# The pool mixer in plain fp32: averaging and mixer products, token reciprocals on the bands, diagonals on ACT, and the first row broadcast ahead of the second slot

## The reference

```
mods = silu(c) @ ada_w + ada_b ; sh1, sc1, g1, sh2, sc2, g2 = split(mods, 6)     # six rows of 1024
u    = rms_norm(x, mix_pre_g) * (1 + sc1) + sh1
for g, win in enumerate((2, 4, 8, 16)):                                          # 4 groups of 256 channels
    y_g = (centred_window_mean(u_g, win) - u_g) @ pool_w[g]                      # 512x256 @ 256x256
y    = concat(y_g) * pool_scale
x    = x + g1 * rms_norm(y, mix_post_g)
f    = conv_ffn(rms_norm(x, ffn_pre_g) * (1 + sc2) + sh2, ...) ; x = x + g2 * rms_norm(f, ffn_post_g)
```

## Time and profile before

| | us |
|---|---|
| median of 3 runs (1765.6 to 1768.2) | 1767.69 |
| the profiled execution, its own time | 1768.48 |
| its span | 1766.8 |
| PE busy in the span | 1672.8 (95%) |
| DVE busy in the span | 1025.7 (58%) |

### The profile page before, as it was taken

The page is one execution under the profiler, slowest core; times in us unless marked ns, Lnnn a source line. Parts: engine busy times, 40 slices in busy tenths (PEclk is TensorE's granted clock), DMA queues, the critical chain, the costliest instruction groups (busy, mean ns, idle before and its releaser), DMA issues.

```text
span 1766.8 us, 22021 instructions
## 1 busy us (share of the span) xinstructions
PE 1672.8 (95%) x8559; PEld 1402.8 (79%) x8559; DVE 1025.7 (58%) x1649; ACT 643.4 (36%) x1021; POOL 240.8 (14%) x746
## 2 busy tenths in 40 slices
PE   5559999999998999999999999999989999999998
PEld 5448888888877888878888888888878888888886
DVE  6898766676665878857333337666716733333223
ACT  5154433332344766745222222333214522222222
POOL 2001610000017766630000000000010000000000
PEclk7669999999999999999999999999989999999999
DMA  7832222344342222223222234567744232223332
GB/s 289 342 137 96 96 96 95 96 124 145 101 117 81 69 67 69 66 86 111 96 96 96 95 96 132 141 191 228 233 125 132 96 98 101 100 96 96 95 96 72
DMA packets 137783, 211.63 MB, mean 120 GB/s; under 512 B 29920, under 2 KB 104016, under 8 KB 134352
## 3 DMA queue, kind: packets, MB, share of 16 engines
q1 hardware_dynamic: 123024, 203.94, 36.0%
q10 hardware_dynamic: 14656, 6.29, 1.3%
HBM read 192.38 MB, written 17.82 MB: 119 GB/s over the span
## 4 chain that ended last, share of the span: by engine, by line
PE 82%; DVE 9%; DMA 3%; issue 2%; ACT 2%; SPq 1%; POOL 0%; ACTq 0%; DVEq 0%; POOLq 0%
PE bank L1805 26%; PE bank L1806 25%; PE bank L1807 25%; DVE ada L1209 1%; DVE prob L1377 1%; ACT prob L944 1%; DVE w_lo L1113 1%; PE bank L1936 1%; PE bank L1845 1%; PE bank L2226 1%; DVE prob L1392 1%; DMA u_scratch<-us 1%; SPq L676 1%; DMA raw<-in_fox_in 1%; DVE gsig L1363 1%
## 5 line engine op out<-in xcount | busy, mean ns | idle before, releaser
L1805 PE MATMUL bank<-hh,w_hi 128*128 128x512 f32 (+1 forms) x1440 | 553.7, 384 | 6.2 <-DVE w_lo L1113 2.5
L1806 PE MATMUL bank<-hl,w_hi 128*128 128x512 f32 (+1 forms) x1440 | 550.1, 382 | 0.0
L1807 PE MATMUL bank<-hh,w_lo 128*128 128x512 f32 (+1 forms) x1440 | 549.9, 382 | 0.0
L1113 DVE TENSOR_TENSOR w_lo<-raw,w_hi 128x1024 fp32r<-128x1024 f32 x264 | 317.7, 1223 | 190.3 <-ACT w_hi L753 187.9
L753 ACT ACTIVATE w_hi<-raw 128x1024 fp32r<-128x1024 f32 x264 | 277.8, 1056 | 388.5 <-PE bank L1807 127.5
L1805 PEld LDWEIGHTS bank<-hh,w_hi 128*128 128x128 f32 x1440 | 273.2, 190 | 60.9 <-DVE w_lo L1113 4.3
L1807 PEld LDWEIGHTS bank<-hh,w_lo 128*128 128x128 f32 x1440 | 273.0, 190 | 52.3
L1806 PEld LDWEIGHTS bank<-hl,w_hi 128*128 128x128 f32 x1440 | 273.1, 190 | 50.6
L1805 PE MATMUL bank<-w_hi,hid 128*128 128x512 f32 x528 | 206.8, 392 | 0.0
L1807 PE MATMUL bank<-w_hi,hid 128*128 128x512 f32 x528 | 205.6, 389 | 0.0
L1806 PE MATMUL bank<-w_lo,hid 128*128 128x512 f32 x528 | 205.5, 389 | 0.0
(11 more groups left out here) (281 smaller groups left out, 2015.7 us busy)
## 6 DMA issues: line engine op xcount, KB each, us to landing
raw<-in_up SPq DMA_DIRECT2D x132, 512.0 KB, 3.3
raw<-in_dn SPq DMA_DIRECT2D x60, 512.0 KB, 3.9
ada<-in_ada_w SPq DMA_DIRECT2D x24, 1024.0 KB, 6.9
raw<-in_fox_in SPq DMA_DIRECT2D x32, 512.0 KB, 3.4
raw<-in_s_w SPq DMA_DIRECT2D x24, 512.0 KB, 4.2
q_scratch<-q_tab SPq DMA_DIRECT2D x8, 512.0 KB, 4.2
w_scratch<-w_new SPq DMA_DIRECT2D x8, 512.0 KB, 5.1
raw<-in_fox_out SPq DMA_DIRECT2D x8, 512.0 KB, 3.5
```

The source lines that it names most:

```text
L1113: dve.tensor_tensor(w_lo[:, n % RING, :], raw[:, n % RING, :], w_hi[:, n % RING, :].bitcast(F32), ALU.subtract).then_inc(lo_done, 1)
L1805: pe.matmul(dst, w_h, r_h, start=first, stop=False, skip_group_check=True)
L1806: pe.matmul(dst, w_h, r_l, start=False, stop=False, skip_group_check=True)
L1807: return pe.matmul(dst, w_l, r_h, start=False, stop=last, skip_group_check=True)
```

## The change

In the averaging, ACT multiplies the four blocks' bands by the tokens' reciprocals (`band_n`, 128 by 576 each), and PE multiplies `xt` by `band_n` in plain fp32: 32 multiplications. `xr_hi`, `xr_lo`, `band_hi` and `band_lo` are gone. ACT takes the result out as `v` in float32; DVE adds the correction to it. The mixer product multiplies `v` by `raw` in plain fp32, 4 multiplications for each block and slot; the scaled `raw` is used as it is, and the two `hi` and two `lo` of slots 0 and 1 are gone (DVE's scaling now counts up `lo_done`). The two diagonals `diag_gpost1` and `diag_amp2` are made by ACT, in eight instructions each. On PE, `bc(0, ...)` moves from between blocks 1 and 2 of slot 1 to ahead of block 0. On DVE, `early_half(0)` moves behind `modulation(3)` and `scaled(amp2, ...)`.

```diff
                     act.activation(dst[:, HALF * h:HALF * h + HALF], bank[b0 + h][:, :], ACT.Copy).then_inc(bc_done, 1)
+
+            def diagonal(dst, cols):
+                for k in range(KT):
+                    part = act.activation(dst[:, k, :], ident[:, :], ACT.Copy, scale=cols[:, k:k + 1])
+                part.then_inc(diag_done, 1)
 
...
                 prime(ACT.Sqrt)
-                act.wait_ge(band_done, 1)
-                for v in (0, 2):
-                    act.activation(band_hi[:, v, :, :], band_f[:, v, :, :], ACT.Copy).then_inc(bandh_done, 1)
                 for b in range(TB):
...
                 for b in range(TB):
-                    act.activation(xr_hi[:, b, :], xt[:, b, :], ACT.Copy, scale=rn2[:, b:b + 1]).then_inc(xr_done, 1)
-                for n in range(2):
-                    hi(S_POOL + n)
+                    act.activation(band_n[:, b, :, :], band_f[:, BAND_OF[b], :, :], ACT.Copy, scale=rn2[:, b:b + 1])\
+                       .then_inc(bandn_done, 1)
                 act.wait_ge(mod_done, 1)
-                act.wait_ge(bandl_done, 2)
                 for k in range(KT):
                     act.wait_ge(win_mm, k + 1)
-                    act.activation(hh[:, k, :], bank[(k + 4) % 8][:, :], ACT.Copy, scale=amp1[:, k:k + 1]).then_inc(vh_done, 1)
+                    act.activation(v[:, k, :], bank[(k + 4) % 8][:, :], ACT.Copy, scale=amp1[:, k:k + 1]).then_inc(v_done, 1)
+                act.wait_ge(mod_done, 2)
+                diagonal(diag_gpost1, gpost1)
                 squares_a(0, S_POOL)
                 bc_copy(0, gpost, 2)
+                act.wait_ge(mod_done, 3)
+                diagonal(diag_amp2, amp2)
                 bc_copy(1, gpre, 4)
...
                     return
-                dve.wait_ge(hi_done, n + 1)
+                dve.wait_ge(hi_done, n + 1 - S_UP1)
                 dve.tensor_tensor(w_lo[:, n % RING, :], raw[:, n % RING, :], w_hi[:, n % RING, :].bitcast(F32),
...
                 dve.reciprocal(rn2[:, :], std2[:, :]).then_inc(r_x, 1)
-                for i, v in enumerate((0, 2)):
-                    dve.wait_ge(bandh_done, i + 1)
-                    dve.tensor_tensor(band_lo[:, v, :, :], band_f[:, v, :, :], band_hi[:, v, :, :].bitcast(F32),
-                                      ALU.subtract).then_inc(bandl_done, 1)
-                dve.wait_ge(r_x, 1)
-                for b in range(TB):
-                    dve.wait_ge(xr_done, b + 1)
-                    dve.wait_ge(xt_done, b + 1)
-                    dve.scalar_tensor_tensor(xr_lo[:, b, :], xt[:, b, :], rn2[:, b:b + 1], xr_hi[:, b, :].bitcast(F32),
-                                             ALU.mult, ALU.subtract).then_inc(xl_done, 1)
                 dot_parts(0, (2, 3))
...
                         .to_broadcast([P, 2, 2, 2 * P])
-                    dve.tensor_tensor(w, w, g, ALU.mult).then_inc(pool_ws, 1)
-                lo(S_POOL)
-                lo(S_POOL + 1)
-
-                def low_v(k):
-                    dve.wait_ge(vh_done, k + 1)
-                    dve.scalar_tensor_tensor(hl[:, k, :], bank[(k + 4) % 8][:, :], amp1[:, k:k + 1],
-                                             hh[:, k, :].bitcast(F32), ALU.mult, ALU.subtract).then_inc(v_done, 1)
+                    dve.tensor_tensor(w, w, g, ALU.mult).then_inc(lo_done, 1)
 
                 def edges(half):
-                    own.settle()
                     dve.wait_ge(v_done, 4 * half + 4)
                     for e in range(2):
-                        part = hl[:, 4 * half:4 * half + 4, e * (T - EDGE):e * (T - EDGE) + EDGE]
-                        dve.tensor_tensor(part, part.bitcast(F32), corr[:, 4 * half:4 * half + 4, e, :], ALU.add)\
-                           .then_inc(corr_done, 1)
-                for k in range(KT):
-                    low_v(k)
+                        part = v[:, 4 * half:4 * half + 4, e * (T - EDGE):e * (T - EDGE) + EDGE]
+                        dve.tensor_tensor(part, part, corr[:, 4 * half:4 * half + 4, e, :], ALU.add).then_inc(corr_done, 1)
                 dot_parts(1)
...
                                               rs[:, e, :, :].unsqueeze(2).to_broadcast([P, 4, 2, EDGE]), ALU.mult))
+                own.settle()
                 edges(0)
                 edges(1)
                 dot_parts(2)
                 modulation(2)
                 scaled(gpost1, G1, "mix_post_g", 0.0)
-                diagonal(diag_gpost1, gpost1[:, :])
+                dve.sem_inc(mod_done, 1)
                 dot_parts(3)
-                early_half(0)
                 modulation(3)
                 scaled(amp2, SC2, "ffn_pre_g", 1.0)
-                diagonal(diag_amp2, amp2[:, :])
+                dve.sem_inc(mod_done, 1)
+                early_half(0)
                 boundary(0, S_UP1)
...
                 pe.wait_ge(xt_dve, TB)
-                pe.wait_ge(band_done, 2)
+                pe.wait_ge(band_done, 1)
                 for e, j in enumerate((PAD, P)):
                     dst = bank[0][:, 4 * EDGE * e:4 * EDGE * e + 4 * EDGE].rearrange("p (g r) -> p g r", g=4)
                     mm = pe.matmul(dst, ones_f[:, :], band_f[:, 2 * e, :, j:j + EDGE], start=True, stop=True)
                 mm.then_inc(rs_mm, 1)
                 pe.wait_ge(rs_done, 1)
-                pe.wait_ge(bandl_done, 2)
                 for blk in range(TB):
-                    pe.wait_ge(xl_done, blk + 1)
-                    v = (0, 1, 1, 2)[blk]
+                    pe.wait_ge(bandn_done, blk + 1)
                     lo_c, hi_c = (PAD if blk == 0 else 0), (BAND - PAD if blk == TB - 1 else BAND)
                     t0 = P * blk - PAD + lo_c
                     for k in range(KT):
-                        cols = slice(P * k, P * k + P)
-                        dst = bank[(k + 4) % 8][:, t0:t0 + hi_c - lo_c]
-                        w, w_low = band_hi[:, v, k // 2, lo_c:hi_c], band_lo[:, v, k // 2, lo_c:hi_c]
-                        if v == 1:
-                            pe.matmul(dst, xr_hi[:, blk, cols], w, start=False, stop=False, skip_group_check=True)
-                            pe.matmul(dst, xr_lo[:, blk, cols], w, start=False, stop=False, skip_group_check=True)
-                            continue
-                        mm = passes(dst, xr_hi[:, blk, cols], xr_lo[:, blk, cols], w, w_low, blk == 0, blk == TB - 1)
+                        mm = pe.matmul(bank[(k + 4) % 8][:, t0:t0 + hi_c - lo_c], xt[:, blk, P * k:P * k + P],
+                                       band_n[:, blk, k // 2, lo_c:hi_c], start=blk == 0, stop=blk == TB - 1,
+                                       skip_group_check=True)
                         if blk == TB - 1:
...
                 pe.wait_ge(corr_done, 4)
+                bc(0, diag_gpost1, 2)
                 for b in range(2):
                     pool_slot(1, b, bank_b(0, b)[:, :]).then_inc(blk_mm, 1)
-                bc(0, diag_gpost1, 2)
                 pe.wait_ge(bc_done, 2)
...
                         w = slice(2 * P * (2 * g + k), 2 * P * (2 * g + k) + 2 * P)
-                        mm = passes(dst[:, 2 * P * g:2 * P * g + 2 * P], hh[:, 4 * s + 2 * g + k, cols],
-                                    hl[:, 4 * s + 2 * g + k, cols], w_hi[:, s, w], w_lo[:, s, w],
-                                    g == 0 and k == 0, g == 1 and k == 1)
+                        mm = pe.matmul(dst[:, 2 * P * g:2 * P * g + 2 * P], v[:, 4 * s + 2 * g + k, cols], raw[:, s, w],
+                                       start=g == 0 and k == 0, stop=g == 1 and k == 1, skip_group_check=True)
                 return mm
```

More of the change, by code:

```diff
@@ L104 @@
 EDGE = 8
+BAND_OF = (0, 1, 1, 2)
 class Tally:
@@ L221, in build @@
         diag_amp2 = in_hid("diag_amp2", [KT, P], F32, 5 * D)
-        xr_hi = in_hid("xr_hi", [TB, D], F32R, 4 * D)
-        xr_lo = in_hid("xr_lo", [TB, D], F32R, 8 * D)
+        band_n = in_hid("band_n", [TB, 4, BAND], F32, 8 * D)
         rs = in_hid("rs", [2, 4, EDGE], F32, 13 * D + 896)
@@ L235, in build @@
         junk_x = in_h("junk_x", [D], F32, KT * T - D)
-        band_hi = at("band_hi", [3, 4, BAND], F32R, whi_at + 4 * 2 * SW)
-        band_lo = at("band_lo", [3, 4, BAND], F32R, raw_at + 4 * 2 * SW)
+        v = in_h("v", [KT, T], F32, 0)
         NP_ = P * QB * (QB + 1) // 2
@@ L326, in build @@
         r_x = sem("r_x")
-        xr_done = sem("xr_done")
+        bandn_done = sem("bandn_done")
         diag_done = sem("diag_done")
@@ L330, in build @@
         bc_done = sem("bc_done")
-        xl_done = sem("xl_done")
         xt_dve = sem("xt_dve")
@@ L336, in build @@
         band_done = sem("band_done")
-        bandh_done = sem("bandh_done")
-        bandl_done = sem("bandl_done")
-        pool_ws = sem("pool_ws")
         win_mm = sem("win_mm")
-        vh_done = sem("vh_done")
         v_done = sem("v_done")
@@ L750, in hi @@
                 act.wait_ge(raw_full[n % RING], RAW_LANDED[n])
-                if n < S_UP1:
-                    act.wait_ge(pool_ws, n + 1)
```

(3 more changed lines are left out.)

## The result

The changed kernel takes 1756.71 us (median of four runs, 1754.55 to 1758.01) against 1767.95 (four runs, 1765.6 to 1768.44): a ratio of 0.9936, 95% interval 0.9923 to 0.9949. That is 11.2 us less. The forecast was 1753.3 and 14.4 us of gain in the profile.

What follows compares the result with a forecast made beforehand. PE bounds the span, but DVE, then ada_w's transfers, set when its dense work starts. Row broadcast 1 12.6 us earlier plus 1.8 from its clock make 14.4 us: median 1753.3, range 1750.5 to 1759.5.

Steps and rivals of the forecast that it cites:

- Scaling of the weights: DVE, scaling of raw: a new 1.8 us wait for scale_bc, scaling until 32.2, wait hidden almost wholly by row 1's landing.
- Row 1: DVE's products of ada_w's row 1: follow the transfers and end at 42.4 instead of 53.83, 11.4 us earlier.
- Row 1 to row 3: Unchanged chain on SP's queue (small loads, row 3's parts): 21.9 us, so row 3 ends at 64.3.
- Row 3 to the mark: Modulation and amp2 0.5, then early_half 2.45 beside ACT's diagonals: 3.0 us, so row broadcast 1 starts at 67.3.
- the mark: Start of row broadcast 1 on PE: from 79.90 to 67.3, 12.6 us earlier; what it moves, the end moves.
- Row broadcast 1 at the higher clock: PE hardly pauses before row broadcast 1, which runs at 2.4 GHz: 1.9 us for 3.75, another 1.8 gained.
- the forecast's own path: The predicted case without any rival: 1753.3 us, own range 1750.5 to 1756.5, chance 0.80.
- the first rival: PE's clock stays down, slot 1 ends at 72.9, row broadcast 1 gains only 6.9 us: 1760.8, chance 0.12.
- The price of plain fp32: PE, one pass of 256 columns: taken as 0.43 us at 1.2 GHz, between 0.21 and 0.76.
- Slot 1 becomes the bound: Row broadcast 1 waits for PE's slot 1, ending at 72.9 if the clock stays down: 1760.8, chance 0.12.
- Stationary loads in the open: Each PE pass of 256 columns pays its load, 0.76 us; slot 1 ends at 83.5: slower, 1771.3, chance 0.04.
- The gain is lost behind the mark: Something later than 114 us (a transfer, POOL's tables) stands still and PE waits for it: 1767.7, chance 0.04.

Runs made afterwards that it cites:

- the repeat: The changed kernel unaltered, timed again beside two later versions: median 1756.09 us of six runs, ratio 0.9941 to the kernel before.
- half of the change alone: Kernel before with only the averaging in plain fp32 (1763.46 us) or only the mixer product in plain fp32 (1759.47 us); diagonals and row broadcast 0 as before.

## Why the prediction was right

The mechanism was right: DVE's work on low parts set the start, it went, and the transfers of `ada_w` came late next. The chain of waits of the changed kernel shows it (start, duration, what ran):

```profile
7.91 17.57 DMA gain_scratch<-vec_t
...
27.49 13.19 DMA ada<-in_ada_w
...
53.55 9.37 DMA ada<-in_ada_w
...
66.05 2.50 DVE ya L1128 x4
...
68.58 2.07 PE bank L1871 x16
```

The store of the gains took 17.6 us to land, and the loads of row 1 were issued behind it. Up to 40.7 us and again from 53.5 us the chain stands on landings. Between the two, cut here, it runs over DVE, which goes through the end of row 1, `edges` and row 2 without a pause. The last part of row 3 was issued at 53.55, when DVE had used the last part of row 2, and it landed behind three parts that SP had issued only from 50.23 us on. With the small loads out of their way DVE met row 3 without a wait, so it was the queue and not that last issue which held row 3. The 14.4 us of the sum came out as 13.0. By its steps:

- **Scaling of the weights.** The wait for `scale_bc` was 3.24 us, not 1.8: row 0 ended at 26.3 us and not 27.5 (ACT's squares and the reciprocal came earlier, at 21.58 against 22.76; in the repeat the wait was 2.41 us). It cost nothing, as predicted: the scaling ended at 32.4, the first part of row 1 landed at 32.5. Where that wait went (row 1 ahead of the scaling) the gain came from the earlier issue.
- **Row 1: mis-sized, 0.7 us.** It ended at 43.08, not 42.4. The first part landed at 32.5 as worked out. The second, issued at 26.36, took 9.4 us where 8.5 were read from the earlier trace rows, and landed at 35.7 instead of 35.1; the others followed at 2.5 us each. In the kernel before no further part stood behind it, and here two do. Whether that is the cause was not tried.
- **Row 1 to row 3: 22.25 us, not 21.9.** The chain over the small loads is there, as their move showed. The last part landed 19.8 us behind row 1's end (19.6 in the sum), and DVE needed 2.4 us for it, not 2.3.
- **Row 3 to the mark: 3.25 us, not 3.0.** `early_half` began 0.7 us behind row 3 and not 0.5. The diagonals on ACT took 2.45 us and were ready 0.2 us ahead of `ya`. Putting them back on DVE moved the mark by 0.5 us, and not by the 1.2 that the sum had for one of them; one execution does not settle this term.
- **Row broadcast 1 at the higher clock: 1.70 us gained, not 1.8.** It took 2.05 us at 2.4 GHz. The step held, and neither half of the change alone has it.

So 0.7 + 0.35 + 0.25 at the mark and 0.1 behind it make the 1.4 us. The rest of the distance between 1753.3 and 1756.71 is the 0.9 of scatter in the tail and 1.3 of time outside the span (1.7 us before, 3.0 in this execution, 1.7 to 3.0 in the later ones), less 0.2 because the median lies a little further below the profiled execution than was worked out; the repeat of the same kernel gave 1753.7 of span and 1756.09 as its median.

The stated range of 1750.5 to 1759.5 holds 1756.71, but the part that belonged to the forecast's own path ended at 1756.5. The strip above had been left for the first rival, which did not come true. That the range held owes something to luck; the repeat's 1756.09 lies inside the narrower part.

**The price of plain fp32.** 256 columns at 2.4 GHz, from the changed kernel's line of the mixer product (ns min/median/max):

```profile
L2019 PE MATMUL bank<-raw,v x64: 379/379/794, 33.9 to 67.7; 128*128 128x256 f32 x64
```

Sixteen passes took 3.72 us, 0.23 each: at 2.4 GHz that is about two cycles a column in each of two passes. The value taken, 0.43 us at 1.2 GHz, is right too: from 44.80 to 47.36 us, with the granted clock at 0.50, six passes took 2.56 us. The records of neighbouring passes overlap: each lasts 379 to 794 ns, longer than what a pass costs.

Of the two rules of the Trainium skill, the one of four passes for true FP32 (FP8 and Floating Point Precision, TensorE Precision Notes) agrees with those four cycles a column. By its other rule (Perfetto Trace Analysis, Engine Utilization), if plain fp32 were the mode FP32_LOW_HIGH, a pass would have taken half as long, an estimated 0.11 us; the trace has 0.23.

**The rivals.** *Slot 1 becomes the bound* was nearer than its 0.12 says. Row broadcast 0 and slot 1 together ran from 56.71 to 68.09 us, 11.4 us where 10.7 were worked out, and ended 0.5 us ahead of the mark instead of 1.1. As soon as DVE was 2 us faster (small loads moved), slot 1 did set the mark, so the margin of half a microsecond was in part luck. It did not decide here because the clock came up within the pair, though later than the 3.9 us behind its start that were taken from the earlier trace rows: it stood at 0.50 until 60 us and at 0.55 on the mean over the next 2, so it rose at about 61.8, 5.1 us behind. The rival's argument against itself, that fp32r ran at narrow columns and plain fp32 brought the clock up, is only half of it: in the kernel before the clock also came up in fp32r (last section). *Stationary loads in the open* was wrong: a pass at 1.2 GHz costs 0.43 us with its load hidden, against the 0.65 from which it would have turned. *The gain is lost behind the mark* was wrong too: 11.3 us at the mark and 13.0 at the start of the dense work came out as 12.1 us of span, with nothing standing still.

**The transfers.** The stretch from 60 to 62 us, which has that clock too (third from last), and the rate of the queue at its end:

```profile
60.00:62.00 2.00, 2.00 (x8) 1.70 (x7) 1.59 (x5) 1.08 (x2) 0.00 (x0) 0.55 1.03 434
```

The queue moved 434 GB/s over these 2 us, where the earlier trace rows had 423 over 14, and the parts of row 1 landed 2.5 us apart. The Trainium skill (Perfetto Trace Analysis, Engine Utilization) gives 358 GB/s as a core's share when both cores of a pair use the memory, and about 435 GB/s in all for the 16 DMA engines of a core that is active alone. This program runs on one core, and the trace agrees with the second figure.

**Left open.** Why the second part of row 1 lands 0.6 us later, and why the granted clock, with which the tail scatters by 4.7 us, stays down longer in some executions.

## What to carry to other kernels

When an engine sheds work at the start of a kernel, follow its inputs next: two halves that gained 4.9 and 7.9 us alone gained 11.3 together, because the loads, issued behind a store that they don't need, came late. Then move the issues: it gave another 4 us for a few lines; small loads that stood ahead of urgent ones had held these up by 2. Look for what is missing from the sum of two halves where both act: here, at the end of row 1. Before you trust an engine's slack, work it out to its next wait: PE had 7 us to spare ahead of 44 us and half a microsecond at 68.

## What the runs showed of the hardware

The granted clock in the averaging, in stretches of 2 us of the changed kernel (PEclk is third from last):

```profile
26.00:28.00 2.00, 2.00 (x11) 2.00 (x11) 0.64 (x4) 0.00 (x0) 0.00 (x0) 0.58 0.75 164
28.00:30.00 2.00, 2.00 (x19) 2.00 (x18) 0.00 (x0) 0.00 (x0) 0.00 (x0) 1.00 1.00 320
```

Before, PE started on the averaging in fp32r at 25.65 us and went from it into the mixer product at 42.75, busy without a pause to 47.4. In stretches of the kernel before:

```profile
25.65:42.75 17.10, 17.10 (x80) 17.10 (x81) 16.52 (x23) 7.87 (x11) 0.00 (x0) 0.50 0.71 277
42.75:46.10 3.35, 3.35 (x17) 3.35 (x18) 3.35 (x6) 0.93 (x2) 0.00 (x0) 0.50 0.00 0
46.10:47.40 1.30, 1.27 (x10) 1.06 (x9) 1.30 (x3) 0.00 (x0) 0.00 (x0) 0.95 0.00 0
```

So it worked for some 20 us at 0.50, and the clock came up only inside the mixer product, about 3.4 us behind its start. In plain fp32 PE had worked some 5 us when the clock came up, at about 28 us, so that the averaging took 10.3 us where 15 were the worst case. The prediction had costed it at nothing, and gained nothing more from it.

Pauses of PE and the length of the row broadcast behind them: 0.50 us and 2.05; 2.42 and 2.05; 2.57 and 2.74; 5.00 and 3.75; 7.09 and 3.75. So the clock outlived a pause of 2.4 us in one kernel and was partly down behind one of 2.6 in another.
